# Four rearrangements at the stage boundaries of a hybrid decoder step

## The reference

```python
proj = jnp.einsum('bld,dc->blc', x, w_in)
z_s, xbc, dt_pre, u_m, v_m, o_m, i_pre, f_pre = jnp.split(proj, offs, axis=-1)
xbc, new_ssd_conv = _causal_conv(xbc, st_ssd_conv, conv_ssd_w, conv_ssd_b)
xbc = jax.nn.silu(xbc)
u_c, new_mconv = _causal_conv(u_m, st_mconv, conv_m_w, conv_m_b)
u_c = jax.nn.silu(u_c)
...
mix = jnp.einsum('blc,cd->bld', jnp.concatenate([y_s, h_m], axis=-1), w_out)
x1 = _layer_norm(ALPHA * x + mix, ln1_g, ln1_b)
x2 = _layer_norm(ALPHA * x1 + _peer(x1, peer_wq, peer_keys, peer_u, peer_v), ln2_g, ln2_b)

def _layer_norm(x, g, b):
    mu = xf.mean(-1, keepdims=True)
    var = jnp.square(xf - mu).mean(-1, keepdims=True)
    return (xf - mu) * lax.rsqrt(var + LN_EPS) * g + b
```

## Time and profile before

| what | value |
|---|---|
| median of 3 runs | 3424.15 us (3408.26, 3424.15, 3424.18) |
| the profiled execution's own time | 3417.68 us |
| its span | 3415.8 us |
| PE busy | 3118.2 us (91%) |
| VectorE busy | 2546.0 us (75%) |
| GpSimd busy | 1710.7 us (50%) |
| ScalarE busy | 933.5 us (27%) |
| moved by DMA | 1074.44 MB, mean 315 GB/s |

### The profile page before, as it was taken

One profiled execution on the slowest core, in us unless ns is written; L12 is line 12 of the kernel. 1 busy time (PEld: TensorE's weight loads), 2 busy tenths in 40 slices (PEclk: granted clock), 3 DMA queues, 4 the chain that ended last, 5 costly groups with the idle time before them and its releaser, 6 DMA issues.

```text
span 3415.8 us, 42585 instructions
## 1 busy us (share of the span) xinstructions
PE 3118.2 (91%) x13811; PEld 2060.5 (60%) x13811; DVE 2546.0 (75%) x5375; ACT 933.5 (27%) x2140; POOL 1710.7 (50%) x1420
## 2 busy tenths in 40 slices
PE   8998999998888888889877658999999999999998
PEld 8997887787333233333244336767667766776774
DVE  6672044888397889998889977777777777777777
ACT  3212222665111121121178771111111111111111
POOL 3231221443036777777754556555555555555553
PEclk9999999999899999999989788999999999999999
DMA  4325465677568999999989999999999999999996
GB/s 147 98 70 171 155 222 191 228 266 286 205 205 314 358 379 373 389 380 358 369 323 348 338 351 392 391 385 395 372 386 396 369 387 378 392 402 388 391 394 240
DMA packets 385759, 1074.44 MB, mean 315 GB/s; under 512 B 55688, under 2 KB 145576, under 8 KB 379280
## 3 DMA queue, kind: packets, MB, share of 16 engines
q0 software_dynamic: 186624, 679.56, 52.5%
q1 hardware_dynamic: 149104, 309.77, 25.3%
q10 hardware_dynamic: 49824, 82.58, 6.5%
HBM read 978.55 MB, written 93.08 MB: 314 GB/s over the span
## 4 chain that ended last, share of the span: by engine, by line
PE 45%; DVE 11%; DMA 9%; issue 5%; POOL 2%; ACT 1%; SPq 0%; DVEq 0%; POOLq 0%; ACTq 0%
PE PB L2260 18%; PE PB L2247 14%; DMA vbf<-in_peer_v,gixv 5%; PE PB L2223 4%; PE PB L2287 3%; PE PB L2236 3%; DVE ub L1916 3%; DMA x1d<-in_peer_u 3%; PE PB L2205 1%; DMA ub<-in_peer_u,gix 1%; POOL vbf L1646 1%; DVE ohb L1863 1%; POOL ub L1646 1%; DVE oha L1861 1%; PE PB L2331 1%
## 5 line engine op out<-in xcount | busy, mean ns | idle before, releaser
L1646 POOL DMA_INDIRECT ub<-in_peer_u,gix x640 | 696.3, 1088 | 725.8 <-DVE hid L1916 525.5
L2260 PE MATMUL PB<-vbd,wd 128*128 128x512 f32 x1536 | 685.0, 596 | 0.0
L2247 PE MATMUL PB<-xds,uts 128*128 128x384 f32 x3072 | 569.5, 340 | 0.0
L2247 PEld LDWEIGHTS PB<-xds,uts 128*128 128x128 f32 x3072 | 531.8, 189 | 0.5 <-issue 0.5
L1646 POOL DMA_INDIRECT vbf<-in_peer_v,gix x340 | 396.4, 1166 | 167.1 <-issue 98.0
L2260 PEld LDWEIGHTS PB<-vbd,wd 128*128 128x128 f32 x1536 | 284.1, 192 | 309.6 <-issue 309.6
L2287 PE MATMUL PB<-vbf,dg 128*64 128x512 f32 x1200 | 319.1, 655 | 96.9 <-DMA vbf<-in_peer_v,gixv 92.2
L1646 POOL DMA_INDIRECT vbf<-in_peer_v,gixv x300 | 324.6, 1082 | 156.4 <-issue 85.0
L1877 DVE TENSOR_TENSOR uts<-PB,uts 128x512 fp32r<-128x512 f32 x256 | 175.6, 686 | 303.0 <-ACT uts L2093 302.7
L1916 DVE CUSTOM_DVE_ANT_0 ub<-ub,x1g 128x1024 f32<-128x1024 f32 x257 | 312.9, 1221 | 47.2 <-DMA ub<-in_peer_u,gix 37.8
L2093 ACT CAST uts<-PB 128x512 fp32r<-128x512 f32 x256 | 149.9, 586 | 646.9 <-PE PB L2236 635.3
(11 more groups left out here) (400 smaller groups left out, 5030.4 us busy)
## 6 DMA issues: line engine op xcount, KB each, us to landing
vbd<-in_peer_v SPq DMA_DIRECT2D x128, 512.0 KB, 6.9
x1d<-in_peer_u SPq DMA_DIRECT2D x96, 512.0 KB, 9.3
gd_d<-stag ACTq DMA_DIRECT2D x12, 2048.0 KB, 9.6
gbd<-gd_d SPq DMA_DIRECT2D x16, 1536.0 KB, 18.9
ubd<-in_peer_u SPq DMA_DIRECT2D x32, 512.0 KB, 10.1
wtr<-in_w_tok SPq DMA_DIRECT2D x6, 2048.0 KB, 9.2
tok_d<-stg ACTq DMA_DIRECT2D x48, 256.0 KB, 2.0
rb_e<-rows_d SPq DMA_DIRECT2D x8, 1536.0 KB, 10.7
```

The lines of the kernel that those rows point to most:

```text
L1646: pool.indirect_dma_start(out=buf, out_offset=None, in_=a[table], in_offset=bass.IndirectOffsetOnAxis(ap=index, axis=0)).then_inc(done, 16)
L2247: last = T.matmul(PB[:, 6, 0:TD], uts[:, b % 2, ul, k, :], xds[:, xl, k, :], start=(k, n) == (0, 0), stop=(k, n) == (KD - 1, 2))
L2260: last = T.matmul(PB[:, 2 * d + n, :], wd[:, b % 2, d * CH:(d + 1) * CH], vbd[b % 8][:, n * 512:(n + 1) * 512], start=b == 0, stop=b == NB ...
```

## The change

Four places are altered.

Start: SP issues seven of the eight `x_t` loads ahead of the two `w_ch` loads, and the low part of the row weights is made on VectorE instead of GpSimd.

Channel loop: ScalarE's work on a block is cut in two functions, the evacuation (`chan_out`) and the SiLU with its stores (`chan_silu`), and a block's SiLU comes behind the next block's evacuation. The 14 row stores are issued after three of ten iterations.

Token products: in the first group of nine units the `w_product` units are 4, 6, 7, 8 instead of 2, 4, 6, 8, and the activation of the sample rows comes two units later.

End: the samples' v rows for b = 4 to 7 are fetched within the loop (t = 650 to 653), ahead of the last gathered v rows. The samples' product is spread over four column groups (each gets two columns of `wgs`). The samples' x1 rows are loaded by eight small DMAs earlier in the dense loop. The closing norms take the row sum from the adding instruction itself (`accum_out`), and mean, squares and root on ScalarE; the samples' norm covers 128 partitions, and their output goes out in two stores.

```diff
+def pick_tiles(j):
+    return () if j >= NHC // 4 else (2, 4, 6, 8) if j else (4, 6, 7, 8)
...
                     sp.dma_start(wrow, a["w_row"]).then_inc(s_wr, 16)
-                    for q in range(2):
-                        sp.dma_start(wcr[q][:, :, :], a["w_ch"][q, :, :, :]).then_inc(s_w[q], 16)
                     for k in range(KD):
                         free(sp, s_xl, k - NX + 1)
                         sp.dma_start(xst[k % NX], a["x_t"][:, k, :]).then_inc(s_x[k % NX], 16)
+                        if k == KD - 2:
+                            for q in range(2):
+                                sp.dma_start(wcr[q][:, :, :], a["w_ch"][q, :, :, :]).then_inc(s_w[q], 16)
...
+                    def chan_pair(i):
+                        chan_out(i, 1)
+                        chan_silu(i, 0)
+                        chan_out(i + 1, 0)
+                        chan_silu(i, 1)
+
+                    chan_out(0, 0)
+                    for i in range(3):
+                        chan_pair(i)
                     act.wait_ge(s_rr, 1)
...
+                    for i in steps(act, NCT // 2 - 1, 3):
+                        chan_pair(i)
+                    chan_out(NCT // 2 - 1, 1)
+                    for q in range(2):
+                        chan_silu(NCT // 2 - 1, q)
...
+                            if t == 1:
                                 act.wait_ge(s_su[q], i + 1)
-                                nc.scalar.activation(stg[b][0:NSMP, :], ssum[:, :], func).then_inc(s_sf[q], 1)
+                                nc.scalar.activation(stg[9 * q % 6][0:NSMP, :], ssum[:, :], func).then_inc(s_sf[q], 1)
...
                     pool.wait_ge(s_wr, 16)
-                    split(wrp, wrow, s_rh, s_rp, 1)
+                    pool.sem_inc(s_go, 1)
+                    nc.gpsimd.tensor_copy(wrp[0][:, :, :], wrow).then_inc(s_rh, 1)
...
+                    dve.wait_ge(s_rh, 1)
+                    nc.vector.tensor_tensor(wrp[1][:, :, :], wrow, wrp[0][:, :, :].bitcast(f32), ALU.subtract).then_inc(s_rp, 1)
...
                         load_xs(4)
+                        sp.wait_ge(s["x1t"], NP)
+                        for n in range(NSMP):
+                            sp.dma_start(x1[32 * (n % 4) + n // 4:32 * (n % 4) + n // 4 + 1, :], x1_d[SEQ + n:SEQ + n + 1, :]).then_inc(s["xsr"], 16)
...
-                            V.scalar_tensor_tensor(y, vbf[:, v % NB, :], wg[:, hv % 2, col:col + 1], y, ALU.mult, ALU.add).then_inc(s["ax"], 1)
+                            total = ends[:, 0, 0:1] if v == U_SLOTS - 1 else None
+                            V.scalar_tensor_tensor(y, vbf[:, v % NB, :], wg[:, hv % 2, col:col + 1], y, ALU.mult, ALU.add, accum_out=total).then_inc(s["ax"], 1)
...
+                def last_sum(n, x, psum):
+                    V.scalar_tensor_tensor(x, x, ALPHA, psum, ALU.mult, ALU.add, accum_out=ends[:, n, 0:1]).then_inc(s["ends_sum"], 1)
+
+                def last_norm(n, x):
+                    dve.wait_ge(s["ysq"], GATHERED + n)
+                    ch.link(V.reciprocal(ends[:, n, 1:2], ends[:, n, 1:2]))
+                    ch.link(V.scalar_tensor_tensor(x, x, ends[:, n, 0:1], gb1[:, :], ALU.add, ALU.mult))
+                    V.scalar_tensor_tensor(x, x, ends[:, n, 1:2], gb2[:, :], ALU.mult, ALU.add).then_inc(s["y"], 1)
...
+                    S.activation(ends[:, n, 0:1], ends[:, n, 0:1], ACT.Copy, scale=-1.0 / D).then_inc(s["ends_mean"], 1)
+                    act.wait_ge(s["ends_mean"], 2 * n + 1)
+                    S.activation(work[:, 0:D], x, ACT.Square, bias=ends[:, n, 0:1], accum_out=ends[:, n, 1:2]).then_inc(s["ends_mean"], 1)
+                    act.wait_ge(s["ends_mean"], 2 * n + 2)
+                    S.activation(ends[:, n, 1:2], ends[:, n, 1:2], ACT.Sqrt, scale=1.0 / D, bias=epsc[:, :]).then_inc(s["ysq"], 1)
...
-                            for x in range(2):
-                                last = T.matmul(PB[0:NSMP, 6 + x, :], wgs[:, n, :], (vbf if n < NB else ub)[:, n % NB, x * 512:(x + 1) * 512],
-                                                start=n == 0, stop=n == NSMP - 1)
+                            for x in range(2):
+                                for g in range(4):
+                                    last = T.matmul(PB[32 * g:32 * g + 2, 6 + x, :], wgs[:, 4 * r + g, 0:2], (ub if r else vbf)[:, g, x * 512:(x + 1) * 512],
+                                                    start=r == 1, stop=r == 0, tile_position=(0, 32 * g))
```

122 lines of the change are left out of this document (59 added, 63 removed).

## The result

| | before | after |
|---|---|---|
| median of 4 runs | 3421.9 us (3408.26 to 3424.18) | 3382.36 us (3379.45 to 3384.62) |
| span of the profiled execution | 3415.8 us | 3382.7 us |
| PE busy | 3118.2 us (91%) | 3107.0 us (92%) |

The ratio is 0.9884, with a 95% interval of 0.9858 to 0.991: the changed kernel is 39.5 us faster by the medians and 33.1 us by the two profiled spans.

The account below looks back on a forecast made before the run. PE, busy 91% of the span, was taken as the bound. Gains of 2.6 + 8.0 + 13.1 + 7.8 = 31.5 us gave 3386.2 us from the profiled execution and 3392.7 from the median; forecast 3389.5, range 3374 to 3406.

Parts of the forecast that it names:

- The start: Kernel start: first x part lands two loads earlier, so PE begins near 6.9 us; gain 2.6 us, bounds 1.0 to 2.8.
- The channel loop: Phase 1: copy ahead of the SiLU removes PE's 5.9 us wait and 2.1 us of slow clock; gain 8.0 us.
- VectorE is late there because of the row maxima: Channel loop near 67 us: row maxima delay VectorE's convolution, for which ScalarE stands at a SiLU ahead of its copy.
- After that VectorE (four passes of some 1.3 us a block) catches up: Channel loop behind PE's stop near 80 us: VectorE catches up with PE, which takes 11.3 us a block.
- The row stores: Channel loop: 14 stores take 6 us of ScalarE, hidden near 98 to 104 us; without cover they cost 6 us.
- Loop to tokens: First nine token units: ScalarE reaches the samples near 270 instead of 284.7 us; gain 13.1 us, lower bound 9.3.
- The end: Behind the last sum into acc: four sums, five norms and 0.75 us of waits; gain 7.8 us, bounds 6.0 to 8.3.
- The samples' loads: Dense loop on SP: eight new loads take 3.4 us of issue, covered by 20 us of slack; cost nothing.
- if phase 3's start to its last block is longer than now: Sign against the prediction: a longer stretch from phase 3's start to its last block would prove it wrong.
- Gains given back in phase 3: Rival: phase 3's gathers absorb phase 1's gains, leaving the end alone; 3413 us, chance 0.09.
- Half of the boundary lost: Rival: between channel loop and token products only half is gained, a later w_product waiting; 3396 us, chance 0.11.
- Slower by SP's wait: Rival: in the dense loop SP waits for x1t and eight loads, delaying u loads over 20 us; 3445 us, chance 0.04.

Follow-up runs that it names:

- e7: Changed kernel with the start as before (channel weights loaded ahead of x, low row weights on GpSimd); ratio to before 0.9904, unit 9 at 302.21 us.
- e8: Changed kernel with only the order of the start's loads as before, low row weights still on VectorE; ratio to before 0.991, unit 9 at 302.45 us.
- e3: Changed kernel with ScalarE's old channel-loop order and the 14 row stores behind the loop; ratio to before 0.9933, unit 9 at 313.11 us.
- e12: e4 with GpSimd's low channel weights cut to an eighth of the columns from the second iteration (work left out); ratio to before 0.9881.
- e2: Kernel before with only the third phase of the changed kernel; ratio to before 0.9977, 3442.45 against 3448.98 us, unit 9 at 335.51 us.
- e4: Changed kernel with ScalarE's old channel-loop order, row stores still after three of ten iterations; ratio to before 0.997, unit 9 at 328.06 us.
- e1: Changed kernel with its third phase (samples' gathers, product, closing norms) as before; ratio to before 0.9902, 3416.1 against 3449.0 us.
- e11: Changed kernel run again unaltered; ratio to before 0.9891, median 3381.7 against 3425.97 us.
- e5: Changed kernel with only the 14 row stores moved back behind the channel loop; ratio to before 0.9913, 3414.68 us, unit 9 at 300.82 us.
- e6: Changed kernel with w_products at units 2, 4, 6, 8 and the samples' activation taken right away; ratio to before 0.9899, 3408.68 us.
- e9: Changed kernel with the eight sample-row loads on SP issued twelve times, 96 in all; ratio to before 0.996, PE waits 23.1 us.

## Why the prediction was right, and where not

**The start** (forecast 2.6, profiles 2.5): the number is partly luck. On another chip the change gives 1.1 to 1.6 (e7, e8). Both loads ahead of `x` cost what was forecast at PE's first matmul, but the profile of before had the clock come late, which made its row products a microsecond longer, and the low part of the last `x` (1.83 us, beside GpSimd) now holds the end, as the forecast had allowed in its bounds of 1.0 to 2.8.

**The channel loop** (8.0, and 8.0 in the pair): the mechanism of the wait, ScalarE standing at a SiLU ahead of the copy, is confirmed by e3, where it returns with the old order alone. Two steps were incomplete. "VectorE is late there because of the row maxima": without GpSimd's passes it would not be late enough, as e12 has no stall near 80. And "After that VectorE (four passes of some 1.3 us a block) catches up": the profile of before does show this up to 120 us, but from there the convolution takes 7.1 to 7.6 us a block beside GpSimd and the chain of copy, convolution, SiLU and stores only just fits into PE's 11.3. In e2, which is the old phase 1 unchanged, it doesn't fit: it takes 11.8 us or more a block, and the split of the token weights costs PE another 11.7 us. There the loop's piece is (275.1 - 22.5) - (247.5 - 21.1) = 26 us instead of 8, partly set off by the nine units behind it, 60.4 us (275.1 to 335.51) instead of 66.7. e12 shows for e4, which runs the same course, that it is GpSimd's work that keeps it so. In e1, on the chip of e2, phase 1 gave 33 us. That the medians of the first comparison differ by 39.5 where the profiles differ by 33.1 fits with some executions of the kernel before taking the slower course, and so do the 44.3 us of e11 (33.1 and the 11.0 between the courses are 44.1); no profile of such an execution was made on those chips, and the intervals are wide, so this stays an inference.

**The row stores** ("Without this cover they would cost their 6 us"): wrong. With the old order they cost 15 us at unit 9 (e4 against e3), as they push the chain out of step. With the new one, nothing (e5).

**Loop to tokens** (13.1; 12.9 and a window of 53.75 us): the sum was right, the reasons were partly idle. The new order gives back the 2.4 us of waiting for the last evacuation, and it brings ScalarE to the samples early enough with either the early stores or the later units; each of them alone can go (e5, e6).

**The end** (7.8; 8.7 on VectorE, less 0.7 for the last stores, so 8.0): five norms of 2.71 came as written. (The forecast's own terms, 8.3 less 0.4, give 7.9.) The waits were 0.9 instead of 0.75, and a sum with its read took 1.13 where nothing had to be waited for (3366.61 to 3367.74), not 1.33, as the read lies inside the instruction's end. The samples' product took 2 x 1.90 and a wait of 0.96 for rows, 4.8 us and not 1.9: the sixteen matmuls in the earlier trace rows are only its `ub` half, and as many with `vbf` stand ahead of them. It still came 1.3 us ahead of need. The rule of the Trainium skill that a scalar_tensor_tensor with two SBUF sources that aren't bf16 runs at half throughput ("Vector Engine (DVE) Microarchitecture Reference", "Points that are easy to get wrong") does not show: the four last sums take 5.44 us whether the last of them accumulates or not, and one with such sources takes 1.28. The row of L1916 that the forecast set against the rule was a weaker test, as it is another instruction.

**The samples' loads** (nothing): right, but with 8 us of slack and not 20 (e9).

**The signs.** All came, but so did one that speaks against the forecast: "if phase 3's start to its last block is longer than now" was met by the first profile: 2503.7 us against 2501.2. e11 has 2497.6, so this sign was set finer than that stage's scatter of 6 us and tells nothing.

**The rivals.** Gains given back in phase 3: out by e11 and the table. Half of the boundary lost: out by the window. Slower by SP's wait: its place is right, its threshold would be 8.3 us and not 20.
